# Six weight chunks of two input projections as seven block products instead of eight, with the sums on VectorE

## What is computed

```python
g  = u @ a_w_in[:, 1536:2560]     # 512 tokens x 1024 x 1024, layer a, gates
k  = u @ b_w_in[:, 1024:2048]     # 512 x 1024 x 1024, layer b, keys
v  = u @ b_w_in[:, 2048:3072]     # 512 x 1024 x 1024, layer b, values
```

## Time and profile before

| | us |
|---|---|
| median of 3 runs | 1249.45 (1248.51 to 1252.17) |
| the profiled execution, its own time | 1246.61 |
| its span, from the first to the last instruction | 1244.8 |
| TensorE busy | 1195.1 (96%) |
| VectorE busy | 445.9 (36%) |
| ScalarE busy | 303.2 (24%) |
| mean granted TensorE clock, share of full | 0.984 |

### The profile page before, as it was taken

One profiled execution on the slowest core, in us unless ns is written; L12 is line 12 of the kernel. 1 busy time (PEld: TensorE's weight loads), 2 busy tenths in 40 slices (PEclk: granted clock), 3 DMA queues, 4 the chain that ended last, 5 costly groups with the idle time before them and its releaser, 6 DMA issues.

```text
span 1244.8 us, 14543 instructions
## 1 busy us (share of the span) xinstructions
PE 1195.1 (96%) x5792; PEld 643.8 (52%) x5792; DVE 445.9 (36%) x1112; ACT 303.2 (24%) x699; POOL 23.1 (2%) x33
## 2 busy tenths in 40 slices
PE   4999999989999999999999899999999999999996
PEld 2446445654465445766887467444444444444442
DVE  3121008971261000394499833222222222222223
ACT  0000008880150001373240433111111111111112
POOL 0000000000001000020000000000000000000000
PEclk9999999999999999999999898999999999999998
DMA  9851515003263232448536767899999999999991
GB/s 343 315 203 68 203 68 203 2 2 135 99 239 93 70 112 88 148 86 272 204 118 220 270 210 285 347 429 426 428 428 428 429 428 429 429 428 429 428 421 44
DMA packets 82034, 311.36 MB, mean 250 GB/s; under 512 B 18097, under 2 KB 18940, under 8 KB 69178
## 3 DMA queue, kind: packets, MB, share of 16 engines
q1 hardware_dynamic: 78384, 309.56, 63.4%
q10 hardware_dynamic: 3386, 0.86, 0.3%
q0 software_dynamic: 208, 0.17, 0.1%
HBM read 309.40 MB, written 1.18 MB: 249 GB/s over the span
## 4 chain that ended last, share of the span: by engine, by line
PE 86%; DVE 9%; DMA 2%; ACT 1%; issue 1%; SPq 1%; DVEq 0%; ACTq 0%
PE ps L1026 18%; PE ps L655 14%; PE ps L1058 9%; PE ps L787 9%; PE ps L651 6%; PE ps L992 5%; PE ps L1004 4%; DVE G L1778 4%; PE ps L737 3%; PE ps L751 3%; PE ps L599 3%; PE ps L724 3%; PE ps L693 3%; PE ps L876 2%; PE ps L828 2%; DMA ring<-in_a_w_in 2%
## 5 line engine op out<-in xcount | busy, mean ns | idle before, releaser
L655 PE MATMUL ps<-U,ring 128*128 128x512 f32 (+1 forms) x608 | 208.1, 503 | 0.0
L1026 PE MATMUL ps<-ring,prob 128*64 128x512 f32 x704 | 188.1, 592 | 1.2 <-issue 1.2
L655 PEld LDWEIGHTS ps<-U,ring 128*128 128x128 f32 x608 | 115.4, 190 | 87.7 <-issue 80.8
L1026 PEld LDWEIGHTS ps<-ring,prob 128*64 128x64 f32 x704 | 61.8, 137 | 100.3 <-issue 100.3
L787 PE MATMUL ps<-U,ring 128*128 128x256 f32 (+1 forms) x384 | 111.6, 451 | 0.0
L787 PEld LDWEIGHTS ps<-U,ring 128*128 128x128 f32 x384 | 72.5, 190 | 37.3 <-issue 31.0
L1942 DVE TENSOR_TENSOR prob<-ps,prob 128x512 f32<-128x512 f32 x16 | 17.2, 1075 | 193.7 <-PE ps L1026 193.7
L651 PE MATMUL ps<-ring,U 128*128 128x512 f32 (+1 forms) x224 | 83.1, 531 | 0.0
L1058 PE MATMUL ps<-ring,prob 128*64 128x512 f32 x352 | 78.0, 595 | 0.0
L1026 PE MATMUL ps<-K,prob 128*64 128x512 f32 x160 | 70.3, 592 | 0.0
L992 PEld LDWEIGHTS ps<-bias,U 128*128 128x128 f32 x512 | 60.8, 198 | 13.4 <-issue 13.4
(11 more groups left out here) (283 smaller groups left out, 1336.6 us busy)
## 6 DMA issues: line engine op xcount, KB each, us to landing
ring<-in_w_exp_gate SPq DMA_DIRECT2D x22, 2048.0 KB, 18.3
ring<-in_w_exp_up SPq DMA_DIRECT2D x20, 2048.0 KB, 16.2
ring<-in_w_exp_down SPq DMA_DIRECT2D x20, 2048.0 KB, 19.2
ring<-in_w_ada SPq DMA_DIRECT2D x12, 2048.0 KB, 12.7
ring<-in_w_mod SPq DMA_DIRECT2D x12, 2048.0 KB, 8.3
ring<-in_b_w_in SPq DMA_DIRECT2D x8, 2048.0 KB, 8.4
ring<-in_a_w_in SPq DMA_DIRECT2D x5, 2048.0 KB, 17.9
ring<-in_w_in SPq DMA_DIRECT2D x5, 2048.0 KB, 10.8
```

The costliest lines, as they stand in the source:

```text
L655: last = mm(ps[:, b, 0:wid], w[:, col:col + P], src[:, k, 0:wid], start=(k == 0), stop=(k == KT - 1))
L1026: last = mm(ps[x * CAP:(x + 1) * CAP, 2 + i, :], xg[:, k, x * CAP:(x + 1) * CAP], chunk(n, 2 * i + x, turn)[0][:, k, :], start=(k == 0), s ...
```

## The change

For six chunks (layer a's two gate chunks, layer b's two key and two value chunks) the product of a 1024x512 chunk with 512 tokens is cut into 2x2 blocks over rows of the weights (the sum) and tokens and over columns of the weights. Eight block products would make the four blocks of the result. The changed kernel makes seven products of sums of blocks (the form of Winograd) and joins them with seven additions. A chunk is two units of 128 of each 256 output columns; a unit has seven products of 4 matmuls of 256 columns, in the order 1, 2, 6, 7, 5, 4, 3, in banks that go round as before.

VectorE makes four sums of tokens a stage, four sums of weights a chunk (each 128x1024), and joins: 7 operations of 128x256 a unit, six of which read PSUM. ScalarE copies product 1 to SBUF, and in layer a it applies silu in place after the joins. VectorE's order is written out by hand:

```diff
+PRODUCTS = (1, 2, 6, 7, 5, 4, 3)
+TAKEN = {2: "c11", 6: "u2", 7: "u3", 5: "c22", 4: "c21", 3: "c12"}
+SUMMED = {"a_in": (3, 4), "b_in": (2, 3, 4, 5)}
+DVE_ORDER = {
+    "a_in": ["t2", "t4", (3, "s2"), (3, "s4")] + [("v", t) for t in range(4)]
+    + unit_events(0) + [(4, "s2"), (4, "s4")] + unit_events(1) + unit_events(2) + unit_events(3),
+    "b_in": [("q", m) for m in range(6)] + ["t2", (2, "s2"), ("q", 6), "t4", (2, "s4"), ("q", 7)]
+    + unit_events(0) + [(3, "s2"), (3, "s4")] + unit_events(1) + unit_events(2) + [(4, "s2"), (4, "s4")]
+    + unit_events(3) + unit_events(4) + [(5, "s1")] + unit_events(5) + [(5, "s2"), (5, "s4")]
+    + unit_events(6) + unit_events(7)}
...
+            def seven_products(stage, u):
+                ch, f = SUMMED[stage][u // 2], u % 2
+                taken_a, taken_d = tk[stage, "act"], tk[stage, "dve"]
+                for at_, i in enumerate(PRODUCTS):
+                    g = 7 * u + at_
+                    bank = g % 4
+                    if i == 1 and f == 0:
+                        landed(PLACE[stage][ch])
+                    if g < 4:
+                        pe.wait_ge(taken_d, dve_count(stage, ("v", (g + 2) % 4) if stage == "a_in" else ("q", 4 + g)))
+                    else:
+                        w, j = (g - 4) // 7, PRODUCTS[(g - 4) % 7]
+                        if j == 1:
+                            pe.wait_ge(taken_a, act_count(stage, w, "p1"))
+                        else:
+                            pe.wait_ge(taken_d, dve_count(stage, (w, TAKEN[j])))
+                    if i == 6:
+                        pe.wait_ge(taken_d, dve_count(stage, (ch, "s2")))
+                        pe.wait_ge(taken_d, dve_count(stage, "t2"))
+                    if i == 7:
+                        pe.wait_ge(taken_d, dve_count(stage, (ch, "s4")))
+                        pe.wait_ge(taken_d, dve_count(stage, "t4"))
...
+                    for k in range(4):
+                        last = mm(ps[:, bank, 0:256], still[:, k, f * P:(f + 1) * P], moving[:, k, :],
+                                  start=(k == 0), stop=(k == 3))
+                    last.then_inc(st[stage], 1)
...
+            def join_products(stage, u):
+                p1, u2, u3, u4 = (PARTS[stage][:, i, :] for i in range(4))
...
+                dve.wait_ge(tk[stage, "act"], act_count(stage, u, "p1"))
+                v.tensor_tensor(corner(stage, u, 0, 0), product(2), p1, ALU.add).then_inc(done, 1)
+                v.tensor_tensor(u2, product(6), p1, ALU.add).then_inc(done, 1)
+                have("u2")
+                v.tensor_tensor(u3, product(7), u2, ALU.add).then_inc(done, 1)
+                v.tensor_tensor(u4, product(5), u2, ALU.add).then_inc(done, 1)
+                have("u3")
+                v.tensor_tensor(corner(stage, u, 1, 1), product(5), u3, ALU.add).then_inc(done, 1)
+                v.tensor_tensor(corner(stage, u, 1, 0), u3, product(4), ALU.subtract).then_inc(done, 1)
+                have("u4")
+                v.tensor_tensor(corner(stage, u, 0, 1), product(3), u4, ALU.add).then_inc(done, 1)
```

On VectorE the token sums of layer a follow the modulation of the tokens, and the first chunk's weight sums follow the tenth rope, ahead of the value copies. In layer b it goes:

```diff
-            for m in range(3, KT):
+            for m in range(3, 6):
                 take_q(m)
+            dve.wait_ge(u_ok, 2 * KT)
+            dve.wait_ge(col_done, CHUNKS["ada1"] + 6)
+            token_sums("b_in", "t2")
+            weight_sums("b_in", 2, "s1")
+            weight_sums("b_in", 2, "s2")
+            take_q(6)
+            token_sums("b_in", "t4")
+            weight_sums("b_in", 2, "s4")
+            take_q(7)
+            join_products("b_in", 0)
+            for part in ("s1", "s2", "s4"):
+                weight_sums("b_in", 3, part)
+            join_products("b_in", 1)
             for j in range(KT):
                 dve.wait_ge(scaled, j + 1)
                 v.tensor_scalar(H[:, j, 0:S], H[:, j, 0:S], vc("ln_g", j), vc("ln_b", j), ALU.mult, ALU.add
```

```diff
-                if n - SLOTS == PLACE["b_in"][2]:
+                if n - SLOTS == PLACE["b_in"][5]:
+                    sp.wait_ge(st["b_in"], used["b_in"][5])
                     load_bias(range(4))
+                    sp.dma_start(late_tables, consts_dram[:, CA["dist"][0]:CA["mult"][1]]).then_inc(table_in, 16)
+                if n == PLACE["ada1"][2]:
+                    sp.wait_ge(tk["a_in", "dve"], len(DVE_ORDER["a_in"]))
...
-                    sp.dma_start(cst[:, CF:CR], consts_dram[:, CF:CR]).then_inc(table_in, 16)
+                    for c0, c1 in ((CF, CA["dist"][0]), (CA["mult"][1], CR)):
+                        sp.dma_start(cst[:, c0:c1], consts_dram[:, c0:c1]).then_inc(table_in, 16)
```

More of the change, by code:

```diff
@@ L292, in modrow @@
                 return rows_beside[stage][:, c]
+            if stage == "ada0" and c >= 4:
+                return rows_gate0[:, c - 4, :]
             return rows_after[:, c % 2, :]
@@ L853, in _ @@
                 raw_q(m, range(KT))
-            in_proj("b_in", uT, {"k": T, "g": S}, skip=KT)
-            pe.wait_ge(tk["b_in", "dve"], sum(j[4] == "dve" for j in JOBS["b_in"]))
-            pe.wait_ge(tk["b_in", "act"], sum(j[4] == "act" for j in JOBS["b_in"]))
+            for u in range(8):
+                seven_products("b_in", u)
+            for m in range(KT):
+                n = PLACE["b_in"][6 + m // 4]
+                if m % 4 == 0:
+                    landed(n)
+                if m < 4:
+                    pe.wait_ge(tk["b_in", "dve"], dve_count("b_in", (7, TAKEN[PRODUCTS[3 + m]])))
+                else:
+                    pe.wait_ge(tk["b_in", "act"], 8 + m - 3)
+                for k in range(KT):
+                    last = mm(ps[:, m % 4, 0:S], slot(n)[:, k, (m % 4) * P:(m % 4 + 1) * P], uT[:, k, 0:S],
+                              start=(k == 0), stop=(k == KT - 1))
+                last.then_inc(st["b_in"], 1)
+            pe.wait_ge(tk["b_in", "dve"], len(DVE_ORDER["b_in"]))
+            pe.wait_ge(tk["b_in", "act"], 8 + KT)
             pe.wait_ge(mod_ok, 4)
@@ L1129, in evac_in @@
                 for i, (kind, m, _, _, eng) in enumerate(jobs):
-                    if stage == "a_in" and i == 14:
-                        mod_rows("ada0", (4, 5), (5, 6))
                     if eng == "act":
@@ L1438, in _, with token_sums @@
             modulate(0, range(4, KT))
+            def token_sums(stage, which):
+                ts, done = TOKEN_SUM[stage], tk[stage, "dve"]
+                if which == "t2":
+                    step(v.tensor_tensor(ts[1], token_part(0, 1), token_part(0, 0), ALU.subtract))
+                    settle()
+                    v.tensor_tensor(ts[2], token_part(1, 1), ts[1], ALU.subtract).then_inc(done, 1)
+                else:
+                    step(v.tensor_tensor(ts[3], token_part(1, 1), token_part(0, 1), ALU.subtract))
+                    dve.wait_ge(done, dve_count(stage, "t2"))
+                    settle()
+                    v.tensor_tensor(ts[4], ts[2], token_part(1, 0), ALU.subtract).then_inc(done, 1)
@@ new lines, in weight_sums @@
+            def weight_sums(stage, ch, which):
+                done = tk[stage, "dve"]
+                s1, s2, s3, s4 = (weight_sum(stage, ch, i) for i in (1, 2, 3, 4))
+                if which == "s1":
+                    n = PLACE[stage][ch]
+                    dve.wait_ge(full[n % SLOTS], 16 * (n // SLOTS + 1))
+                    ins = v.tensor_tensor(s1, weight_part(stage, ch, 1, 0), weight_part(stage, ch, 1, 1), ALU.add)
+                    if ch == 5:
+                        ins.then_inc(done, 1)
+                    else:
+                        step(ins)
+                    step(v.tensor_tensor(s3, weight_part(stage, ch, 0, 0), weight_part(stage, ch, 1, 0), ALU.subtract))
+                elif which == "s2":
+                    settle()
+                    if ch == 5:
+                        dve.wait_ge(done, dve_count(stage, (5, "s1")))
+                    v.tensor_tensor(s2, s1, weight_part(stage, ch, 0, 0), ALU.subtract).then_inc(done, 1)
+                else:
+                    dve.wait_ge(done, dve_count(stage, (ch, "s2")))
+                    v.tensor_tensor(s4, weight_part(stage, ch, 0, 1), s2, ALU.subtract).then_inc(done, 1)
@@ L1458, in _ @@
                 if r == 9:
+                    dve.wait_ge(rope_ok, 10)
+                    for part in ("s1", "s2", "s4"):
+                        weight_sums("a_in", 3, part)
                     for t in range(4):
@@ L1662, in _ @@
             take_gates(1)
-            jobs = JOBS["b_in"]
-            for i, (kind, m, _, _, eng) in enumerate(jobs):
-                if eng == "dve" and kind != "q":
-                    dve.wait_ge(st["b_in"], i + 1)
-                    dst = kTb[:, m, :] if kind == "k" else vb[:, m[1], m[0] * 512:(m[0] + 1) * 512]
-                    v.tensor_copy(dst, ps[:, i % 4, :]).then_inc(tk["b_in", "dve"], 1)
+            join_products("b_in", 2)
+            for part in ("s1", "s2", "s4"):
+                weight_sums("b_in", 4, part)
+            join_products("b_in", 3)
```

(7 more changed lines are left out.)

131 lines of the change are left out of this document (104 added, 27 removed).

## The result

The changed kernel took **1229.36 us** (1228.16 to 1232.39, 4 runs) beside 1248.98 us (1246.86 to 1252.17) for the kernel before on the same chip: a ratio of 0.985 (95%: 0.982 to 0.988). The forecast was 1231.2, with 1228.0 to 1236.5 as its range. The profiled execution took 1228.16 us; one like the profile of before was to take 1228.4.

The account below looks back on a forecast made before the run. TensorE's matmul work was taken to bound the kernel: 19.9 - 1.2 - 0.5 = 18.2 us off the profiled 1246.61 gave 1228.4 us, or 1231.2 for a median 2.8 us higher. The range was 1228 to 1236.5 us.

Parts of the forecast that it names:

- TensorE's columns: In both projections, 164.9 us of matmuls are removed and 145.1 us added: a gain of 19.9 us.
- Waits at the starts of products: In the units, each product starts after one to three more waits than a matmul inside a job: no cost taken.
- The rival of the group starts: In the units, first weight loads not fetched ahead cost 0.19 us a product, 16 us in all: 1247.2 us, chance 0.05.
- the slower rival: In the units, many short groups lower the granted clock; at 0.86 the kernel takes 1254.8 us; chance 0.04.
- VectorE's prices: For VectorE's 1024-column sums: 1.22 us each, starting 1.13 us apart, or 1.25 where one needs the other's result.
- The 1.7 us that the estimate gave for the entry: At the second projection's entry, the skill's price of 1.23 us even for independent sums gives 1.7 us loss, against 1.2.
- 36 + 28 - 5.5: VectorE's added work: some 36 + 28 us, less eight evacuations of 0.69 us, beside 145 us of TensorE.
- Slack inside the units: Behind a unit's last product, VectorE's join and four sums end with three us of slack, at three places: no loss.
- Token sums of layer a: In the first stage, the four sums end at 59.9 us, before the first rotation's result is read at 60.67: no loss.
- The term of 1.2 us: At the second projection's entry, product 7 waits for VectorE to take query 7: loss 1.2 us (0.4 to 2.5).
- The end of layer a's gates: Ahead of the first attention, a join and a 128x256 activation come last: loss 0.5 us (0.3 to 1.0).
- The bound of 16.1 us: Behind unit 7, moved bias loads issue, land and are masked in 16.1 us, under 27.6 us of gate jobs: no loss.

Follow-up runs that it names:

- Eight products: The changed kernel with product 3 of every unit computed twice, all sums, joins and transfers kept: 1253.16 us, ratio 1.004 to the kernel before.
- early sums: The changed kernel with layer b's first two weight sums ahead of query 3 and no TensorE wait for the last silu before attention a: 1227.41 us, ratio 0.985.
- transfers alone: The kernel before with only the change's moved bias and table loads and the held modulation chunk: 1248.09 us, ratio 1.001.
- the row alone: The kernel before with ScalarE's last modulation row made ahead of layer b's token tiles: 1244.51 us, ratio 0.998.
- first projection only: The changed kernel with layer b's projection, bias and tables as in the kernel before: 1240.57 us, ratio 0.995.
- early sums and row: The early sums kernel with ScalarE's last modulation row also made ahead of layer b's tokens: 1225.96 us (0.984), again 1224.86 us (0.982).

## Why the prediction was right

**TensorE's columns.** 336 matmuls at 0.4317 us were to take two stretches of 48.4 and 96.7 us. They took 48.47 and, without the entry pause, 96.70. Eight products against seven, with all else equal, cost the 20.7 us.

**Waits at the starts of products.** Taken as nothing. Products start 1.73 us apart wherever no pause is named above, and the stretch of all 448 records in *early sums* is 448 x 0.2158. The rival of the group starts (16 us) is false.

**The clock in the units.** 1.00 in both windows, so the slower rival is false. The Trainium skill (TensorE: Matmul & The Clock Gate, "A second HAM failure mode: psum-queue depth-cycling") reports swings of the clock in a kernel (bf16, 512 columns) that turns through its banks; in 145 us of such work in the changed kernel, four banks turning every 1.73 us, no window shows it.

**VectorE's prices.** The line through the rows of 256 and 512 columns gave 1.22 us length, 1.13 apart and 1.25 when dependent; measured 1.22, 1.14 and 1.25. The Trainium skill (VectorE: DVE Perf Modes, "Side-by-side: where the cycles go for N=2048 bf16") gives a fixed part of about 150 cycles, by which the prediction's estimate was 1.23: that matches the length, and not the spacing of sums that don't depend on each other, which is what a stream of them costs. The 1.7 us that the estimate gave for the entry is as near to the 1.5 measured (below) as the 1.2 taken, but not for its reason: from the end of query 5 to the end of query 7 VectorE took 12.0 us, as worked out with 1.13. VectorE's busy time rose by 65.7 us in all, where the working has 36 + 28 - 5.5 = 58.5: it counted operations by their spacing, the profile by their length.

**Where the sums end last.** Slack inside the units: 3.0 us in the prediction, 2.8 to 2.9 measured by two ways. Token sums of layer a: done at 58.5 us, the first rotation's result read at 59.28, no pause. Entry: the idle time is 1.25 us, at the place named, product 7 of the first unit, and ended by VectorE. The term of 1.2 us was nevertheless too small, for it stood for the whole delay. Product 7 started 1.4 us behind its turn, and from the first product to the second gates TensorE took 98.22 us, where the same records take 96.70 without a pause (*early sums*, 371.01 to 467.71): 1.5 us. The missing 0.3 is what the idle time doesn't count: records that follow each other overlap by 0.16 us (the group of 376.43 us ends 1.89 us later, the next would start 1.73 later), and the first product behind a pause takes 1.99 us in place of 1.89. The place came out although a base of the working moved: the queries ran 1.5 us long, and TensorE and VectorE's taking of query 5 came later together.

**The end of layer a's gates.** 0.5 us; the pause grew from 0.78 to 1.34. The time was right, and one detail not: the silu behind the last join takes the whole tile, 128x512 and not 128x256. It took 0.63 us against the 0.60 assumed.

**Transfers.** Nothing that shows, alone and within the change. The bound of 16.1 us for issue, landing and masks was 10.7, since the issues took 5.37 and ran beside the masks.

**The time.** 18.2 us off the profiled execution were forecast and 18.45 came. That agreement is better than the working deserves. The two stages gave 17.7 where 18.2 was worked out, 0.3 of the difference at the entry and nearly all of the rest in the columns (19.7 for 19.9); stretches beside them gave the rest of the gain, -1.4, +0.2, +1.5 and -1.0, and that they sum to so little is luck. The first goes with the clock and not with the transfers taken out of the start. In the 14 profiles the first gates begin in the chain at 130.5 to 131.0 us in six, all with a clock of 0.97 in the first 60 us, and at 131.6 to 132.2 us in eight, all with 0.94. Eight products and transfers alone have the moved transfers and are among the late ones (132.05 and 132.16); the row alone has the old ones and is among the early (130.70).

**What it left out.** The 2.43 us pause of the earlier trace rows was read as evidence that pauses don't lower the clock, since its window showed 1.00. In six of the ten profiles with that pause it was followed by a fall, and the profile of before happened to be one of the others. It didn't change the forecast, but it belongs to its range: with the same kernel, two chips gave 0.985 and 0.988. The median, 1229.4, lies 1.8 us below the forecast for medians: the profiled execution came 0.2 us below its own, and the median lies 1.2 us above it where 2.8 had been taken from three runs. Those three ran high, or their chip did: the kernel before averages 1247.1 us over 51 executions on four chips.

## What to carry to other kernels

Where the chain is unbroken matmul work and VectorE stays more than half idle beside it even with the sums (36% and 42% busy here), a block product less in eight is worth its columns, all of them, as long as each join and sum ends ahead of the bank that waits for it; count that slack product by product. The places to look at are the borders: the order in which VectorE takes the last results of the stage before and makes the first sums of the next set the larger of the two new pauses. Make the sums of the first chunk early, and give a small operation that another engine waits for its turn ahead of a long sum.

## What the runs showed of the hardware that was not expected

A pause of TensorE can cost more than its length. Behind 2.42 us of waiting, 64 records of 128x258 took 15.65 to 16.95 us in six profiles, and 14.19 or 14.20 in the others; behind 2.84 us, 8 records took 3.68 us in place of 1.99. Behind the 1.25 us at the entry it was not seen, but in the first attention the clock fell in seven of 14 profiles with no pause above 1.34 us ahead and TensorE busy throughout, at a cost of 1.6 us. Kernels with the same work at a place did both there: the kernel before and transfers alone kept 1.00 in the queries, first projection only fell. So a single profile that shows 1.00 proves little. Both profiles of the changed kernel fell at the same places, and so did both of the early sums and row, so it isn't plain chance either. What decides it stays open.

The mean granted clock goes with more than half of the spread of one kernel's time (correcting for it took the standard deviation of 51 executions from 2.3 to 1.5 us): the fastest executions of the kernel before (1242.1 to 1243.1 us) had 0.988 and 0.989, the slowest (1251.9 to 1252.3) 0.979 to 0.982. Where a change is worth a few us, that clock is worth a look beside every time.
